# Small parameter loads and the low-rank weight moved behind the first key tiles, and one activation moved ahead of a weight's high part, in a decoder-layer kernel

## The reference, cut to what matters

```python
mod = jax.nn.silu(c) @ w_ada + b_ada
sh1, sc1, g1, sh2, sc2, g2 = jnp.split(mod, 6, axis=-1)
h = rmsnorm(x, norm_pre1) * (1 + sc1[:, None]) + sh1[:, None]
proj = h @ w_in
bg, cg, ua, q, k, v, r, lr, ga, gb = jnp.split(proj, split_idx, axis=-1)
...
log_a = jax.nn.log_sigmoid((lr @ w_a2 + b_a).astype(jnp.float32)) / GLA_TAU
```

## Time and profile before

| | |
|---|---|
| median of 3 runs | 1012.21 us (1010.62 to 1012.27) |
| span of the profiled execution | 1007.4 us |
| what lies around the span (median less span) | 4.8 us |
| PE busy | 987.9 us, 98% of the span |
| DVE, ACT, POOL busy | 543.0, 385.9, 228.6 us |
| DMA, mean over the span | 115 GB/s |
| granted TensorE clock, mean | 0.999 |

### The profile page before, as it was taken

How to read it: one execution, slowest core, us unless ns; L and a number is a source line. 1 busy time by engine, 2 the same in 40 slices (tenths; PEclk the granted TensorE clock), 3 DMA queues, 4 the chain that set the end, 5 groups by cost and what they waited for, 6 DMA issues and landing times.

```text
span 1007.4 us, 18705 instructions
## 1 busy us (share of the span) xinstructions
PE 987.9 (98%) x7743; PEld 897.7 (89%) x7743; DVE 543.0 (54%) x868; ACT 385.9 (38%) x588; POOL 228.6 (23%) x124
## 2 busy tenths in 40 slices
PE   7799999999999999999999999999999999999997
PEld 5689889999999999899998789999999999888886
DVE  2501104667555665346436688877777778750204
ACT  4532533143343334443463345333333334533212
POOL 2043433233343333233343020000000000013330
PEclk9999999999999999999999999999999999999999
DMA  9565344598366657545427042222322222323212
GB/s 354 171 93 180 116 90 96 129 115 136 106 193 165 138 128 139 91 105 160 123 91 219 1 124 86 64 85 84 85 84 85 84 85 63 126 64 100 79 59 94
DMA packets 144132, 115.59 MB, mean 115 GB/s; under 512 B 11353, under 2 KB 123761, under 8 KB 143025
## 3 DMA queue, kind: packets, MB, share of 16 engines
q1 hardware_dynamic: 143953, 114.38, 43.5%
q10 hardware_dynamic: 96, 0.04, 0.0%
HBM read 107.02 MB, written 7.35 MB: 114 GB/s over the span
## 4 chain that ended last, share of the span: by engine, by line
PE 93%; SPq 2%; DMA 1%; ACT 1%; DVE 1%; issue 1%; DVEq 0%
PE pair L1874 50%; PE pair L1929 16%; PE pair L2250 10%; PE pair L2203 5%; PE pair L2009 1%; PE pair L1982 1%; DMA raw<-in_w_in 1%; PE pair L1861 1%; SPq L667 1%; SPq L705 1%; PE pair L1921 1%; PE pair L2072 1%; PE pair L2061 1%; PE pair L1922 1%; PE pair L1923 1%
## 5 line engine op out<-in xcount | busy, mean ns | idle before, releaser
L1874 PE MATMUL pair<-h_hi,w_hi 128*128 128x288 f32 x1280 | 285.6, 301 | 0.1
L1874 PE MATMUL pair<-h_hi,w_lo 128*128 128x288 f32 x1280 | 279.1, 296 | 0.0
L1874 PE MATMUL pair<-h_lo,w_hi 128*128 128x288 f32 x1280 | 278.8, 295 | 0.0
L860 POOL TENSOR_TENSOR w_lo<-raw,w_hi 128x1024 fp32r<-128x1024 f32 x57 | 140.1, 2459 | 601.5 <-ACT w_hi L931 601.5
L1874 PEld LDWEIGHTS pair<-h_hi,w_hi 128*128 128x128 f32 x1280 | 207.2, 189 | 18.4 <-issue 16.3
L1874 PEld LDWEIGHTS pair<-h_lo,w_hi 128*128 128x128 f32 x1280 | 207.6, 188 | 0.0
L1874 PEld LDWEIGHTS pair<-h_hi,w_lo 128*128 128x128 f32 x1280 | 207.7, 188 | 0.0
L931 ACT ACTIVATE w_hi<-raw 128x1024 fp32r<-128x1024 f32 x70 | 73.5, 1056 | 160.5 <-PE pair L1923 75.7
L860 POOL TENSOR_TENSOR w_lo<-raw_c,w_hi 128x1024 fp32r<-128x1024 f32 x24 | 68.2, 2846 | 124.7 <-ACT w_hi L931 124.7
L1929 PE MATMUL pair<-w_hi,f_hi 128*128 128x512 f32 x176 | 68.9, 391 | 0.0
L1929 PE MATMUL pair<-w_lo,f_hi 128*128 128x512 f32 x176 | 68.7, 390 | 0.0
(11 more groups left out here) (349 smaller groups left out, 1603.5 us busy)
## 6 DMA issues: line engine op xcount, KB each, us to landing
raw<-in_w_in SPq DMA_DIRECT2D x256, 64.0 KB, 3.1
raw_c<-in_w_ada SPq DMA_DIRECT2D x32, 512.0 KB, 5.8
raw_c<-in_w_in SPq DMA_DIRECT2D x192, 64.0 KB, 3.6
raw<-in_w_up SPq DMA_DIRECT2D x24, 512.0 KB, 4.7
raw<-in_w_down SPq DMA_DIRECT2D x22, 512.0 KB, 3.7
raw_up<-in_w_up SPq DMA_DIRECT2D x20, 512.0 KB, 3.8
ada_first<-in_w_ada SPq DMA_DIRECT2D x8, 1024.0 KB, 13.8
raw<-in_w_in SPq DMA_DIRECT2D x8, 512.0 KB, 4.7
```

The source lines that it names most:

```text
L860: pool.tensor_tensor(lo, raw_tile(n)[:, :], hi.bitcast(F32), ALU.subtract).then_inc(S("w_lo_done"), 1)
L1874: ins = pe.matmul(bank[pair][:, half, 0:HALF], w[:, i, :], x[:, i, HALF * half:HALF * half + HALF], start=i == 0 and p == 0, stop=i == KT ...
```

## The change

1. On SP the last six of the 15 small loads leave their places between the `ada_first` blocks and are issued behind key tile 3, ahead of query tile 0.
2. On SP `w_lr` is issued behind key tile 1 and no longer behind key tile 0.
3. On ACT the first block of `h_hi` stands ahead of `high(0)`.
4. On PE `parameters()` waits for nine loads and does one transpose; the other five transposes are in `late_parameters()`, behind query tile 5 of the loop (n = 5). DVE's three copies of them move behind the fourth `z_min`; PE waits for them ahead of the second group of token tiles of the first value tile.

```diff
             for i in range(KT):
                 sp.dma_start(ada_first[:, i, :], w_ada[P * i:P * i + P, 0:2 * D]).then_inc(S(f"ada_in{i}"), 16)
-                for dst, src in small[3 * i:3 * i + 3]:
+                for dst, src in small[3 * i:min(3 * i + 3, 9)]:
                     sp.dma_start(dst, src).then_inc(S("rows_in"), 16)
             load_raw(TILE_K, in_cols(IN_K))
+            load_raw(TILE_K + 1, in_cols(IN_K + DK))
             sp.dma_start(w_lr[:, :, 0:RANK], w_in[:, IN_LR:IN_LR + RANK].rearrange("(k p) c -> p k c", p=P)) \
               .then_inc(S("lr_in"), 16)
-            load_raw(TILE_K + 1, in_cols(IN_K + DK))
...
             for h in range(2, HEADS):
                 load_raw(TILE_K + h, in_cols(IN_K + h * DK))
+            for dst, src in small[9:]:
+                sp.dma_start(dst, src).then_inc(S("rows_in"), 16)
...
-            high(0)
 
             act.wait_ge(S("x_ch"), TT)
             act.wait_ge(S("mul1_done"), 1)
             for i in range(KT):
+                if i == 1:
+                    high(0)
                 act.activation(h_hi[:, i, 0:SEQ], h32[:, i, 0:SEQ], ACT.Identity, bias=mod[:, i, 0:1],
...
-            dve.tensor_copy(ffp[:, :], one_bank(6)[:, P:P + 88]).then_inc(S("prm_done"), 1)
-            dve.tensor_copy(mix0[:, :, :].rearrange("p a j -> p (a j)"), one_bank(7)[:, 0:P]).then_inc(S("prm_done"), 1)
-            dve.tensor_copy(ff0[:, :, :].rearrange("p a j -> p (a j)"), one_bank(7)[:, P:P + 352]) \
-               .then_inc(S("prm_done"), 1)
...
-            dve.wait_ge(S("prm_done"), 4)
+            dve.wait_ge(S("prm_done"), 1)
...
+            dve.wait_ge(S("rows_tr"), 2)
+            dve.tensor_copy(ffp[:, :], one_bank(6)[:, P:P + 88]).then_inc(S("prm_done"), 1)
...
             def parameters():
 
+                pe.wait_ge(S("rows_in"), 16 * 9)
+                pe.wait_ge(S("x_ch"), 4)
+                pe.transpose(one_bank(6)[:, 0:124], rows[0:124, :], ident[0:124, 0:124]).then_inc(S("rows_tr"), 1)
+
+            def late_parameters():
+
                 pe.wait_ge(S("rows_in"), 16 * 15)
-                pe.wait_ge(S("x_ch"), 4)
-                pe.transpose(one_bank(6)[:, 0:124], rows[0:124, :], ident[0:124, 0:124])
+                pe.wait_ge(S("z_min"), 4)
                 pe.transpose(one_bank(6)[:, P:P + 88], rows_ffn[0:88, :], ident[0:88, 0:88])
...
             pe.wait_ge(S("lr_in"), 16)
             pe.wait_ge(S("lr_zero"), 2)
-            pe.wait_ge(S("prm_done"), 4)
+            pe.wait_ge(S("prm_done"), 1)
             pe.wait_ge(S("mod_done"), 1)
...
+                if n == 5:
+                    late_parameters()
...
                     if n == 0 and tiles[0] == 2:
                         pe.wait_ge(S("stacked"), 2)
+                        pe.wait_ge(S("prm_done"), 4)
```

More of the change, by code:

```diff
@@ L1344, in _ @@
                    .then_inc(S("z_min"), 1)
+            dve.wait_ge(S("rows_tr"), 2)
+            dve.tensor_copy(ffp[:, :], one_bank(6)[:, P:P + 88]).then_inc(S("prm_done"), 1)
+            dve.tensor_copy(mix0[:, :, :].rearrange("p a j -> p (a j)"), one_bank(7)[:, 0:P]).then_inc(S("prm_done"), 1)
+            dve.tensor_copy(ff0[:, :, :].rearrange("p a j -> p (a j)"), one_bank(7)[:, P:P + 352]) \
+               .then_inc(S("prm_done"), 1)
             dve.memset(score[:, :, :], 0.0).then_inc(S("zeroed"), 1)
```

## The result

The changed kernel takes 1013.82 us (median of 20 runs, 1011.85 to 1016.04), the kernel before in the same comparison 1011.62 us (20 runs, 1010.51 to 1015.84). The ratio is 1.0021, with a 95% interval of 1.0014 to 1.0029: **2.2 us slower**. A second comparison gave 1.0019 (1.0010 to 1.0029). It was forecast at 1011.7 us, as a change too small to be told; it came out slower, with an interval that does not reach 1, and inside the stated range of 1009.6 to 1015.0.

What follows compares the result with a forecast made beforehand. PE, busy 98%, runs densely from 45.55 us; its start was limited by DMA up to 33 us, then key tile 0. Span 1007.4 - 1.0 + 0.5 = 1006.9, with 4.8 around it 1011.7 us; range 1009.6 to 1015.0.

Steps and rivals of the forecast that it cites:

- the low-rank weight becomes the stall: First key product: PE stands waiting for `w_lr`; landing at 42.3 makes the change 2.0 us slower; chance 0.20.
- The 4.8 us added around the span: Whole run: 4.8 us added to the forecast span of 1006.9 us to give the time of 1011.7 us.
- The six small loads: Front DMA queue: without them the last modulation block and all behind it come 0.9 us earlier.
- ACT's block: ACT ahead of `high(0)`: the first `h_hi` block fills the wait for key tile 0, gaining 0.75 us.
- `w_lr` lands at 39.8: Load behind key tile 1: lands at 39.8 us, bounds 34.7 to 49.7, so the dense stretch starts 1.0 us earlier.
- Five transposes in the dense stretch: PE behind query tile 1: the moved transposes lose their cover and cost 0.5 us, bounds 0.4 to 0.8.
- The covers: SP's late issues delay query tile 0 by 0.4 us under 11 us of cover; DVE's copies fit a gap; both cost nothing.
- the weight stays hidden: First key product: tile 0 lands before 35.9 and `w_lr` by 38, giving -1.7 us, 1010.5; chance 0.25.

Runs made afterwards that it cites:

- the eight kernels above: Four kernels with the six small loads at the front against four without them; the last modulation products start 1.1 us earlier in the mean without.
- e2: Changed kernel with PE's wait for `w_lr` moved from the first key pass to ahead of `lr_rows`; measured again 1009.74 us against 1011.05 before, 0.9989.
- e3: Kernel before with only `w_lr` moved behind key tile 1; 2.6 us slower than before, 1.0026.
- e8: Changed kernel with PE's late wait for `w_lr` and 34 idle transposes instead of 16; no faster than with the late wait alone, time not given.
- e14: Kernel before with only `w_lr` moved behind key tile 1 and PE's wait for it moved to ahead of `lr_rows`; 1010.79 us, 0.9998.
- e6: Changed kernel with 56 idle PE transposes instead of 16; total time not given, first key product at 43.39 us.
- e9: Kernel before with 40 idle PE transposes instead of 16; 0.47% slower.
- e10: Changed kernel with `w_lr` issued from ACT's queue at the program's start; 1013.16 us, 1.0020 against before.
- e11: Changed kernel with `w_lr` issued from ACT's queue at the program's start and 34 idle transposes; 1015.71 us, 1.0040 against before, five executions.
- e1_lr_back: Changed kernel with `w_lr` issued ahead of key tile 1 again; measured again 1009.32 us against 1010.97 before, 0.9978.
- e12: Kernel before with 40 idle transposes instead of 16 ahead of the first key product and the first pass's 24 left out; 1010.51 us, 0.9996.

## Why the prediction was wrong

The time came out 2.1 us above the forecast. What happened is the rival "the low-rank weight becomes the stall", to which I gave 0.20. The 4.8 us added around the span were partly luck of one execution, as said above; since the forecast is the median of before less 0.5, that does not enter it.

1. *The six small loads*, -0.9 us at the front: right. In the changed kernel the products start at 32.51 and not at 32.1, but its first token transposes were at 14.62 where before had 14.08; the eight kernels above put the gain at 1.1 us.
2. *ACT's block*, -0.75 us: right. The first of it ran from 35.66 while the tile was still out, `high(0)` started at 36.90 (36.4 forecast, for the same late front), and ACT was ready for PE at 39.17 (38.8).
3. *`w_lr` lands at 39.8*: **the step that failed.** I put its 64 KB into the queue like as many bytes of key tile 1, and took 1.3 us off the end of the same transfers. It landed at 42.32, 2.5 us later. Key tile 1's own last piece was there at 39.6, about where I had put the end of both; what I had at nothing is the 2.7 us from there to `w_lr`. SP could issue it only at 36.20, since the pieces of the key tiles still went out slowly: the eight of key tile 1 took 8.13 us to issue, where they took 9.89 before. From there it took 6.1 us, in after, `e2`, `e3` and `e8`, with 6.2 in `e14` and 6.8 in `e6`. In the kernel before such a price was hidden: its 10.0 us ended at 37.7, 2.7 us ahead of PE, and only 0.4 us behind key tile 0's last piece at 37.3. That agreement is what I built on, and it did not carry over to the new place.
4. *The clock*: a term that I did not have. The forecast priced a longer stall at its own length. PE's clock was also at 0.50 behind it, and four steps took 1.1 us in place of 0.59: 2.06 us in the profiled execution. The rival said that a landing at 42.3 costs 2.0 us, and it landed there and the medians say 2.2. That this fits so well is in part luck: by the rival's sum the dense stretch would have started at 47.05, and it started at 49.52; the medians differ by less because the kernel before loses some of the same term in most of its other executions.
5. *Five transposes in the dense stretch*, +0.5: right, 0.43 us.
6. *The covers*: right. SP issued the small loads from 51.02 on and query tile 0 at 53.66 (53.00 before), and PE shows no wait for it. DVE's timeline after, for the earlier trace rows, has its idle time of 16.91 us left behind the copies and the memset:

```profile
92.25 0.25 DVE L1345 COPY ffp<-pair 128x88 f32<-128x88 f32 x1 [11.79 <-PE pair L1799]
...
112.71 2.56 DVE L1352 TENSOR_TENSOR pre<-pre,suf 128x2304 f32<-128x2304 f32 x1 [16.91 <-ACT suf L1002]
```

7. *The rival "the weight stays hidden"* rested on key tile 0 being held up by the small pieces behind it. With none behind it, the window of 32 to 34 us still has a share of 0.24 and 57 GB/s, against 0.24 and 62 before, and the tile came at 36.9. That reason fell. Why the DMA engines are slow there is open.

Open as well: what the issue waits at L1982 and L1994 are (none or 0.3 us in before, in both profiles of after and in the first of `e2`; 1.7 to 2.7 us in `e6`, `e8`, `e9`, `e10`, `e14` and the second of `e2`, 3.9 us in two in `e11`). `w_lr` back in its place gains 4.2 us on after (from 1.0019 to 0.9977), but costs only 2.6 us when it alone is moved, though the first product shifts by 3.2 us in both pairs. The clock fits most of that difference of 1.6 us: its mean over the executions is 0.9954 in after and 0.9978 in `e1_lr_back`, 2.4 us of a span, and 0.9969 in before and 0.9957 in `e3_lr_alone`, 1.2 us. Why it falls less in `e1_lr_back` than in before is open.

## What to carry to other kernels

When a load is moved behind others, look for where it is waited for and not only where it is read: here the wait stood ahead of both key tiles' first pass and the use behind it, and with the wait moved as well the change is 2.0 and 1.3 us faster than before (two comparisons) instead of 2.2 us slower. Don't price a load of small pieces by its bytes: the 64 KB in 1024 pieces of 64 B landed 6.1 us after their issue, 2.7 us behind the 64 KB in rows of 512 B issued just ahead, and put the front off by 4.0 us when they stood there. If it matters, measure it at its new place. A wait of an engine whose clock can fall costs more than its length; look at the granted clock of the windows around it before it is put into a sum. And set the profiled execution beside the others: a fast one of the kernel before and a slow one of the kernel after made 5.2 us out of 2.2.

## What the runs showed of the hardware

Around the first key product the granted clock fell (its lowest window of two microseconds has 0.50 in eight profiles, 0.55 and 0.57 in two) with gaps of PE of 2.67 us (`e1` again), 2.86, 2.89, 3.22, 3.25, 3.7, 3.98, 5.66, 5.9 and 6.12 us, and did not after 1.1, 1.46, 2.1, 2.55 and, in the kernel before, 3.29 us. A gap of 3.29 us kept the clock and one of 2.67 us lost it, so the length of the gap alone did not decide it. It also fell after the gaps of 4.68 and 4.76 us at the front of `e10` and `e11`, and stayed at 1.00 through the first microseconds of the program, where PE has nothing to do for 7 us. In `e12`, with a gap of 0.86 us and then five of 0.17 us between its steps, it fell only at 46 to 48 us, to 0.58. While it was down, a step of two products and three transposes took 1.12 us, and at full clock 0.59.

More idle work for PE was no cure: with 40 transposes in place of 16 the clock stayed at 1.00 through the first key tile of the profiled execution, and the kernel was 0.47% slower. Its profiled execution, 1011.9 us, is the fastest of its twelve (up to 1020.65), so it does not show where the rest went.
